# Expert slots filled from both ends: gather products of 160 columns in place of 256, turned one-hots of 132 in place of 260

## The chip, the cores and the metric

The kernel runs on one core of one Trainium2 chip. The metric is the device time in microseconds (us) of one execution. TensorE (PE) runs matrix products; its weight loads (PEld) are instructions of their own that overlap with products. VectorE (DVE) and ScalarE (ACT) read and write SBUF and PSUM; SyncE (SP) issues the DMAs. The granted clock of TensorE is given as a share of 2.4 GHz.

## What is computed

One step of a trunk with two layers over 256 tokens: 128 context tokens (group 0, the prompt) and 128 latent tokens (group 1), each 1024 wide, all in float32. Layer 0 mixes tokens with a convolution module, layer 1 with attention; after either comes the same mixture of experts, and this is what the change touches:

```python
def moe(h, router_w, router_bias, wg, wu, wd, sg, su, sd):
    scores = jax.nn.sigmoid(jnp.einsum('td,de->te', x, router_w, ...))
    ...
    _, eidx = lax.top_k(jnp.where(emask, choice, -jnp.inf), TOP_K)
    wsel = jnp.take_along_axis(scores, eidx, axis=1)
    wsel = wsel / jnp.sum(wsel, axis=-1, keepdims=True) * ROUTED_SCALE
    routed = routed_experts(x, eidx, wsel, wg, wu, wd)
    return (routed + swiglu(x, sg, su, sd)).reshape(B, L, D)
```

Each token goes to 8 of 64 experts; an expert is `(silu(x @ wg) * (x @ wu)) @ wd` with wg and wu of 1024x256 and wd of 256x1024, so its weights are 3 MB. All 64 experts' weights are read in either layer.

## The kernel before

**Routing.** All 256 tokens' scores are computed at once; VectorE picks each token's 8 experts as a 0/1 matrix `sel` (tokens on partitions, 64 experts along the row, one matrix for each token group). TensorE multiplies `sel` with triangular and full matrices of ones (L793 to L797) to get, in PSUM bank `ps[7]`, how many tokens with the same expert stand ahead of each token. VectorE turns this into `rank` (L1565, L1567): the token's slot at that expert, group 0 first and group 1 behind it. An expert has 64 slots. Experts with more tokens than slots get further turns, "overflow" turns, whose number and list VectorE and TensorE work out between L1569 and L1599 (`novc`, `novb`, `ovl`, `table`); TensorE works on the shared expert's hidden rows (L783) between these small steps.

**Pairs.** Experts are worked in pairs, so that two experts' 64 slots fill 128 partitions. There are 32 pairs, and a 33rd for two overflow turns that always runs; further overflow pairs run only where `nov > 2`. Both the 32 pairs and the 33rd run through the same code, `pair`, most of them in a loop of 4 pairs (two pairs' slots, 256 of them, are gathered together). For each pair TensorE does, in this order:

- gate_up (L861): the pair's 128 gathered rows times the gate and up weights, in full float32, 32 instructions of 512 columns; the two experts share the array's columns.
- gather, first half (L834): 8 products. Gathering is itself a product: weights are a 128x128 block of the token rows, split in a rounded float32r part `h_hi` and a float32r rest `h_lo`; the moving operand is `hot`, one-hot columns that say which token stands in which slot. One product covers all 256 slots of two pairs for one token group and one of the parts, so 2 groups x 2 parts add up in PSUM for each of 8 blocks of the width; half of the blocks are done beside one pair, half beside the next.
- combine (L901): 16 products of 256 columns that add the pair before into the 256 tokens' sums.
- hidden_t (L878): two transposes of the hidden rows.
- gather, second half (L834): 8 more products.
- combine_t (L870): the one-hots of the next pair, turned to slots x tokens, by two products with `turn`, a matrix of 260 columns for each token group: identity in the group's own 128 columns, zeros in the other's 128, and 4 columns of routing weights between them. The two products add up in the last 260 columns of bank `PT`.
- down (L890): hidden rows times the down weights, 16 instructions.

ScalarE copies the gathered blocks out (L1204), applies silu (L1210) and writes the rounded part of the pair's output (L1216). VectorE makes the one-hots four pairs ahead (L1612) from `rank` and a row of numbers 0 to 63, copies the routing weights in between the turned identities (L1620), copies the turned one-hots out (L1626), and multiplies silu by up (L1638).

**Weights.** SyncE issues the weights' DMAs into a ring of four experts: when gate_up of a pair has ended, the gate and up weights of the pair two later (4 DMAs of 1 MB, L392), and when its down has ended, the down weights of that pair (2 DMAs of 1 MB, L396). Behind the last expert of layer 0 the same queue carries the 6 MB of the attention's weights (L518) and the first units of 1 MB of the adaLN weights (L368), whose products (L541) are among the first that TensorE does in layer 1.

Of the kernel before, what the change touches and what calls it, by code (L numbers as in the profile page):

```python
# [31 lines left out]
G = 2  # L32
# [16 lines left out]
MAXOVF = TT * TOPK // (SLOTS + 1) + 1  # L49
OVF_PAIRS = MAXOVF // 2  # L50
# [8 lines left out]
TURN = TT + 4  # L59
# [47 lines left out]
def build_kernel(nc, x_prompt, x_sample, cache_k, cache_v, c, c_ctx, ada_w, ada_b, norm_mix, norm_ffn,  # L107
# [4 lines left out]
    with ExitStack() as ctx:  # L112
# [49 lines left out]
        novc = sb("novc", [NE, 8])  # L162
# [20 lines left out]
        eye = rounded("eye", [P, 3 * P + 8], rw_at, 0)  # L183
        turn = [eye[:, 0:TURN], eye[:, P + 4:P + 4 + TURN]]
        wst = eye[:, P:P + 2 * (P + 4)].rearrange("p (g c) -> p g c", g=G)[:, :, 0:4].rearrange(
# [46 lines left out]
        def block_of(i, k):  # L232

            q, second = i // 2 % 2, i % 2
            if q == 0:
                return 8 * second + k
            return 4 * second + k + (4 if k >= 4 else 0)

# [295 lines left out]
        def _(pe):  # L534
# [59 lines left out]
            for l in range(L):  # L594
# [199 lines left out]
                pe.matmul(ps[7][:, NE:2 * NE], ubf[:, 1, :], selb[:, 0, :], start=True, stop=False)  # L794
                pe.matmul(ps[7][:, NE:2 * NE], ubf[:, 0, :], selb[:, 1, :], start=False, stop=True)
                for g in range(G):
                    mm = pe.matmul(ps[7][0:NE, 2 * NE:2 * NE + 2], selb[:, g, :], ubf[:, 1, 0:2],  # L797
                                   start=(g == 0), stop=(g == G - 1))
# [474 lines left out]
        def _(dve):  # L1273
# [67 lines left out]
            for l in range(L):  # L1341
# [213 lines left out]
                if l == 0:  # L1555
                    dve.tensor_scalar(eye[:, P + 4:2 * P + 4], ident, 0.0, None, ALU.mult)
                    for o in (0, 2 * P + 8):
                        dve.tensor_copy(eye[:, o:o + P], ident)
# [241 lines left out]
```

## Time and profile before

| what | value |
|---|---|
| time, median of 3 runs (lowest to highest) | 1396.32 us (1395.77 to 1397.83) |
| time of the profiled execution | 1399.58 us |
| its span, first to last instruction | 1397.8 us |
| PE busy | 1351.7 us, 97% of the span |
| VectorE, ScalarE busy | 449.4 us (32%), 305.6 us (22%) |
| mean granted clock | 0.979 |
| DMA in the 40 slices of the experts' stages | 9 tenths or more, 401 to 424 GB/s |

The profiled execution's own time is 1.8 us above its span, and 3.3 us above the median of the runs. The page gives busy time by engine, the span in 40 slices, the chain of work that ended last, and groups of instructions with their mean duration. An instruction's duration holds the whole way through the engine; products that follow each other overlap, so that what a product costs is read from how far apart their starts are, or from the chain, not from its duration.

### The profile page before, as it was taken

The page shows a single profiled execution, that of the slowest core. Times are in us where ns is not written, and L with a number is a line of the kernel's source. Part 1 is how long each engine was busy: PE and PEld are TensorE (multiplying, and loading weights), DVE is VectorE, ACT ScalarE, POOL GpSimd, SP SyncE. Part 2 cuts the span into 40 slices and gives each one's busy share as a digit, 9 for nine tenths or more (in the row PEclk, how much of TensorE's full clock was granted, in tenths as well). Part 3 has the DMA queues.
Part 4 walks back from the last instruction along what each step waited for, and adds up shares of the span by engine and source line. Part 5 has one row for each costly group of instructions (what it writes and reads, how often), then busy time and mean ns, then how long its engine had stood idle before and what let it go on. Part 6 is the DMA issues. An engine that isn't in the chain of part 4 may idle for free.

```text
span 1397.8 us, 19630 instructions
## 1 busy us (share of the span) xinstructions
PE 1351.7 (97%) x7334; PEld 781.2 (56%) x7334; DVE 449.4 (32%) x1488; ACT 305.6 (22%) x641; POOL 21.1 (2%) x34
## 2 busy tenths in 40 slices
PE   5998999999999999999989999999999999999997
PEld 2776784555555555555534687655555555555554
DVE  1698262222222222222134525222222222222212
ACT  2343231121121111111131423111111111111111
POOL 0041000000000000000000000000000000000000
PEclk8899999999999999999999979999999999999999
DMA  9986879699999999999992726569999999999991
GB/s 346 396 335 276 307 313 370 248 407 418 421 420 418 412 417 418 421 409 424 418 417 88 308 111 251 217 251 401 419 422 421 414 416 414 421 419 408 418 420 65
DMA packets 83011, 499.46 MB, mean 357 GB/s; under 512 B 10697, under 2 KB 19569, under 8 KB 26128
## 3 DMA queue, kind: packets, MB, share of 16 engines
q1 hardware_dynamic: 82384, 498.57, 87.4%
q8 instruction: 31, 0.51, 0.1%
q10 hardware_dynamic: 576, 0.22, 0.1%
q14 instruction: 20, 0.16, 0.0%
HBM read 497.45 MB, written 1.31 MB: 357 GB/s over the span
## 4 chain that ended last, share of the span: by engine, by line
PE 92%; DVE 4%; DMA 2%; issue 1%; ACT 1%; SPq 0%; DVEq 0%; ACTq 0%
PE ps L861 33%; PE ps L890 17%; PE ps L834 10%; PE ps L901 9%; PE ps L566 4%; PE ps L613 3%; PE ps L653 3%; DVE ps L1365 2%; DMA ring<-in_conv_w_dram 2%; PE ps L541 2%; PE ps L783 2%; PE ps L878 1%; PE ps L870 1%; PE ps L719 1%; PE ps L821 1%; PE ps L555 1%
## 5 line engine op out<-in xcount | busy, mean ns | idle before, releaser
L861 PE MATMUL ps<-ring,hT 128*64 128x512 f32 x2048 | 453.3, 594 | 1.2 <-ACT hT L1204 0.9
L861 PEld LDWEIGHTS ps<-ring,hT 128*64 128x64 f32 x2048 | 166.1, 137 | 281.6 <-issue 276.7
L890 PE MATMUL ps<-ring,W 128*64 128x512 f32 x1024 | 233.8, 598 | 1.0 <-DVE W L1643 1.0
L1649 DVE TENSOR_TENSOR ypart<-ps,ypart 128x512 fp32r<-128x512 f32 x132 | 91.3, 692 | 187.1 <-ACT ypart L1216 187.1
L834 PE MATMUL ps<-hot,h_hi 128*128 128x256 f32 x544 | 146.6, 304 | 0.6 <-ACT hT L1204 0.6
L1638 DVE SCALAR_TENSOR_TENSOR vec<-silu_h,W,ps 128x256 f32<-128x256 f32 x66 | 31.7, 480 | 354.7 <-ACT silu_h L1210 354.7
L901 PE MATMUL ps<-comb,ypart 128*128 128x256 f32 x1056 | 138.5, 284 | 0.6 <-DVE ypart L1649 0.6
L890 PEld LDWEIGHTS ps<-ring,W 128*64 128x64 f32 x1024 | 67.8, 136 | 119.5 <-issue 109.6
L834 PE MATMUL ps<-hot,h_lo 128*128 128x256 f32 x544 | 134.4, 281 | 0.0
L1204 ACT ACTIVATE hT<-ps 128x512 f32<-128x512 f32 x136 | 81.2, 597 | 240.3 <-PE ps L834 240.3
L901 PEld LDWEIGHTS ps<-comb,ypart 128*128 128x128 f32 x1056 | 131.4, 191 | 4.2 <-DVE ypart L1649 2.6
L834 PEld LDWEIGHTS ps<-hot,h_hi 128*128 128x128 f32 x544 | 103.1, 189 | 53.0 <-issue 51.9
L1216 ACT ACTIVATE ypart<-ps 128x512 fp32r<-128x512 f32 x132 | 78.9, 598 | 179.8 <-PE ps L890 179.8
L1210 ACT ACTIVATE silu_h<-ps 128x256 f32<-128x256 f32 x66 | 25.4, 385 | 423.3 <-PE ps L861 423.3
L834 PEld LDWEIGHTS ps<-hot,h_lo 128*128 128x128 f32 x544 | 103.0, 189 | 0.1
L1643 DVE COPY W<-ps 128x256 f32<-128x256 f32 x66 | 28.0, 425 | 153.2 <-PE ps L878 153.2
L1365 DVE SCALAR_TENSOR_TENSOR ps<-W,vec,ps 128x256 f32<-128x256 f32 x168 | 66.9, 481 | 0.0
L613 PE MATMUL ps<-hT,ring 128*128 128x256 f32 x256 | 59.7, 394 | 1.5 <-DMA ring<-in_conv_w_dram 1.5
L613 PEld LDWEIGHTS ps<-hT,ring 128*128 128x128 f32 x256 | 50.1, 198 | 13.2 <-issue 3.4
L1626 DVE CAST comb<-ps 128x128 fp32r<-128x128 f32 x132 | 32.2, 286 | 66.4 <-PE ps L870 66.4
L1612 DVE TENSOR_SCALAR hot<-cst,rank 128x64 fp32r<-128x64 f32 x256 | 46.7, 246 | 0.0
L653 PE MATMUL ps<-S,hT 128*128 128x512 f32 x96 | 41.8, 593 | 0.0
(208 smaller groups left out, 914.4 us busy)
## 6 DMA issues: line engine op xcount, KB each, us to landing
ring<-in_exp_w_gate_dram SPq DMA_DIRECT2D x128, 1024.0 KB, 8.3
ring<-in_exp_w_up_dram SPq DMA_DIRECT2D x128, 1024.0 KB, 10.5
ring<-in_exp_w_down_dram SPq DMA_DIRECT2D x128, 1024.0 KB, 10.3
ring<-in_ada_w_dram SPq DMA_DIRECT2D x26, 1024.0 KB, 16.5
S<-in_ada_w_dram SPq DMA_DIRECT2D x22, 1024.0 KB, 13.9
S<-in_attn_wqkv_dram SPq DMA_DIRECT2D x1, 6144.0 KB, 25.5
ring<-in_conv_w_dram SPq DMA_DIRECT2D x4, 1024.0 KB, 19.6
ring<-in_conv_w_dram SPq DMA_DIRECT2D x2, 2048.0 KB, 15.6
```

Of the source, the lines that this page charges most:

```text
L566: mm = pe.matmul(banks[b][:, h * TT:(h + 1) * TT], w[:, k, (2 * b + h) * P:(2 * b + h + 1) * P], x[:, k, :], start=(k == 0), stop=(k == KC ...
L613: mm = pe.matmul(ps[3 + n % 4][:, h * TT:(h + 1) * TT], w1[:, k, h * D + n * P:h * D + (n + 1) * P], hT[:, k, :], start=(k == 0), stop=(k ...
L653: mm = pe.matmul(ps[3 * g + n][:, :], hT[:, k, g * T:(g + 1) * T], wqkv[:, k, n * 512:(n + 1) * 512], start=(k == 0), stop=(k == KC - 1))
L834: mm = pe.matmul(bank[:, kk * TT:(kk + 1) * TT], held, hot[:, buffer, g, :], start=(n == 0), stop=(n == 2 * 2 - 1))
L861: mm = pe.matmul(PGU[64 * b:64 * b + 64, :].rearrange("p (h f) -> p h f", h=2), xg[:, block_of(layout, k), 64 * b:64 * b + 64], gate_up_of ...
L890: mm = pe.matmul(bank[64 * b:64 * b + 64, :], hidT[:, j, 64 * b:64 * b + 64], down_of(w[b])[:, j, n * 512:(n + 1) * 512], start=(j == 0), ...
L901: pe.matmul(acc[k // 2][:, (k % 2) * TT:(k % 2 + 1) * TT], ypart[:, part, k * P:(k + 1) * P], comb[:, par, :], start=False, stop=False, sk ...
L1204: act.activation(blocks[:, lo // step_m:lo // step_m + pairs, lo % step_m:lo % step_m + 2, :], bank[:, :].rearrange("p (k m s) -> p m k s" ...
L1216: act.activation(half_of(0, h), bank[:, :], ACT.Copy).then_inc(act_yhi[l], 1)
L1365: ins = dve.scalar_tensor_tensor(last, x, tap, o, ALU.mult, ALU.add)
L1612: ins = dve.tensor_scalar(hot[:, c // 2 % 2, g, 128 * (c % 2) + 64 * b:128 * (c % 2) + 64 * b + 64], iota, column(rank[:, g, :], 2 * i + b ...
L1649: dve.tensor_tensor(half_of(1, h), bank[:, :], half_of(0, h), ALU.subtract).then_inc(dve_ylo[l], 1)
```

## The change

Slots are given out from both ends. Group 0's tokens of an expert take slots 0, 1, 2 and so on, up to slot 39 at most; group 1's take slots 63, 62, 61 and so on downward, to slot 24 at the lowest, and no lower than group 0's count. So a token group only ever stands in 40 of an expert's 64 slots, and a gather product for one group streams 4 pieces of 40 columns (`spanned`) in place of all 256. What the tokens' groups have beyond that goes to overflow turns, which take 32 more from either group. The turned one-hots of the two groups go to overlapping ranges of 132 columns, so the zero halves of `turn` are left out; the four columns in which they overlap are the weights, that add up as before.

On TensorE the rank products no longer add up the two groups (one count each), and there are as many as before. On VectorE the rank computation grows, and the overflow ranks move behind the first pair's `combine_copy` (`overflow_ranks`).

```diff
+SPAN = 40
+HALF = SLOTS // 2
+OVF_PAIRS = (3 * TT * TOPK // (SPAN + 2 * HALF + 1) + 3) // 4 * 2
+MAXOVF = 2 * OVF_PAIRS
...
-TURN = TT + 4
+TURN = P + 4
...
-                pe.matmul(ps[7][:, NE:2 * NE], ubf[:, 1, :], selb[:, 0, :], start=True, stop=False)
-                pe.matmul(ps[7][:, NE:2 * NE], ubf[:, 0, :], selb[:, 1, :], start=False, stop=True)
+                pe.matmul(ps[7][:, NE:2 * NE], ubf[:, 0, :], selb[:, 1, :], start=True, stop=True)
+                pe.matmul(ps[7][:, 2 * NE:3 * NE], ubf[:, 1, :], selb[:, 0, :], start=True, stop=True)
...
+                def spanned(v, g):
+
+                    at = 0 if g == 0 else SLOTS - SPAN
+                    return v.rearrange("p (e s) -> p e s", s=SLOTS)[:, :, at:at + SPAN]
...
-                            mm = pe.matmul(bank[:, kk * TT:(kk + 1) * TT], held, hot[:, buffer, g, :],
-                                           start=(n == 0), stop=(n == 2 * 2 - 1))
+                            mm = pe.matmul(spanned(bank[:, kk * TT:(kk + 1) * TT], g), held, spanned(hot[:, buffer, g, :], g),
+                                           start=(n == 0), stop=(n == 2 * 2 - 1), skip_group_check=True)
...
-                        mm = pe.matmul(PT[:, 512 - TURN:512], hot[:, buffer, g, 2 * SLOTS * par:2 * SLOTS * (par + 1)],
-                                       turn[g], start=(g == 0), stop=(g == G - 1))
+                        o = 512 - TT - 4 + P * g
+                        mm = pe.matmul(PT[:, o:o + TURN], hot[:, buffer, g, 2 * SLOTS * par:2 * SLOTS * (par + 1)],
+                                       turn[g], start=(g == 0), stop=(g == G - 1), skip_group_check=True)
...
-                dve.tensor_scalar(rank[:, :, :], rank[:, :, :], -1.0, None, ALU.add)
-
-                step(dve.tensor_copy(novc[:, 0:1], ps[7][0:NE, 2 * NE:2 * NE + 1]))
-                for n in range(3):
-                    ins = dve.tensor_scalar(novc[:, 1 + n:2 + n], novc[:, 0:1], (n + 1) * SLOTS + 0.5, None, ALU.is_gt)
+
+                dve.tensor_scalar(lowest, ps[7][:, 2 * NE:3 * NE], float(SLOTS - SPAN), float(SPAN), ALU.max, ALU.min)
+                dve.tensor_scalar(rank[:, 0, :], rank[:, 0, :], -1.0, None, ALU.add)
+                dve.tensor_scalar(rank[:, 1, :], rank[:, 1, :], -1.0, float(SLOTS), ALU.mult, ALU.add)
...
+                dve.tensor_scalar(over[:, 0, :], rank[:, 0, :], SPAN - 0.5, float(SLOTS), ALU.is_gt, ALU.mult)
+                dve.tensor_tensor(over[:, 1, :], lowest, rank[:, 1, :], ALU.is_gt)
...
+                for n in range(4):
+                    ins = dve.tensor_scalar(novc[:, 8 + n:9 + n], novc[:, 5:6], n * HALF + 0.5, None, ALU.is_gt)
                 step(ins)
-                step(dve.tensor_tensor(novc[:, 4:5], novc[:, 1:2], novc[:, 2:3], ALU.add))
-                step(dve.tensor_tensor(novc[:, 4:5], novc[:, 4:5], novc[:, 3:4], ALU.add))
+                step(dve.tensor_reduce(novc[:, 4:5], novc[:, 8:12], AX_X, ALU.add))
...
                 combine_copy(0, 0)
+                overflow_ranks()
```

TensorE inside the experts' loop, second half of a gather and the turned one-hots, before (`hot`: one-hots, `h_hi` and `h_lo`: the token rows' two parts, `eye`: the turned identities, `vec`: the hidden rows):

```order
L878 MATMUL ps<-cst,vec 128x128 x2
L834 MATMUL ps<-hot,h_hi 128x256
L834 MATMUL ps<-hot,h_lo_50 128x256
...
L870 MATMUL ps<-eye,hot 128x260 x2
L890 MATMUL ps<-ring,W 64x512 x8
```

and after:

```order
L892 MATMUL ps<-cst,vec 128x128 x2
L847 MATMUL ps<-hot,h_hi 128x4x40
L847 MATMUL ps<-hot,h_lo_50 128x4x40
...
L884 MATMUL ps<-eye,hot 128x132 x2
L904 MATMUL ps<-ring,W 64x512 x8
```

The order and the number of products stay; the gather products go from 256 columns to 4 pieces of 40, the turned one-hots from 260 to 132.

VectorE in the routing, from the ranks to `novb`, which TensorE waits for (`wt` holds `lowest`), before:

```order
L1565 SCALAR_TENSOR_TENSOR rank<-ps,sel 128x128
L1567 TENSOR_SCALAR rank<-rank 128x128
L1569 COPY novc<-ps 64x1
L1571 TENSOR_SCALAR novc<-novc 64x1 x3
L1573 TENSOR_TENSOR novc<-novc 64x1
L1574 TENSOR_TENSOR novc<-novc 64x1
L1575 TENSOR_SCALAR novb<-cst,novc 64x128
```

and after:

```order
L1578 SCALAR_TENSOR_TENSOR rank<-ps,sel 128x128
L1581 TENSOR_SCALAR wt<-ps 128x64
L1582 TENSOR_SCALAR rank<-rank 128x64
L1583 TENSOR_SCALAR rank<-rank 128x64
L1584 COPY novc<-ps 64x2
L1585 TENSOR_SCALAR W<-rank 128x64
L1586 TENSOR_TENSOR W<-wt,rank 128x64
L1587 TENSOR_SCALAR novc<-novc 64x1
...
L1593 TENSOR_SCALAR novc<-novc 64x1 x4
L1595 TENSOR_REDUCE novc<-novc 64x1
L1596 TENSOR_SCALAR novb<-cst,novc 64x128
```

9 instructions became 18, all ahead of the same `novb`. The 17 instructions of `overflow_ranks` come later, between the first pair's `combine_copy` and its `hidden`, where VectorE had none.

## Rows read from the trace of the kernel before

**Rows 1.** The page, busy time by engine.

```profile
PE 1351.7 (97%) x7334; PEld 781.2 (56%) x7334; DVE 449.4 (32%) x1488; ACT 305.6 (22%) x641; POOL 21.1 (2%) x34
```

**Rows 2.** Chain of one pair in layer 0: start us, us, what.

```profile
403.79 6.98 PE ps L861 x32
410.77 1.15 PE ps L834 x8
...
414.08 0.95 PE ps L834 x8
415.03 0.24 PE ps L870 x2
415.27 3.58 PE ps L890 x16
```

**Rows 3.** The page's groups: xcount | busy us, mean ns | idle before.

```profile
L834 PE MATMUL ps<-hot,h_hi 128*128 128x256 f32 x544 | 146.6, 304 | 0.6 <-ACT hT L1204 0.6
L1638 DVE SCALAR_TENSOR_TENSOR vec<-silu_h,W,ps 128x256 f32<-128x256 f32 x66 | 31.7, 480 | 354.7 <-ACT silu_h L1210 354.7
```

**Rows 4.** Timeline of PEld as a gather begins: start us, us.

```profile
410.70 0.19 PEld L834 LDWEIGHTS ps<-hot,h_hi 128*128 128x128 f32 x1 [0.81 <-issue]
410.81 0.19 PEld L834 LDWEIGHTS ps<-hot,h_lo 128*128 128x128 f32 x1
```

**Rows 5.** Timelines and chain where other products with 128x128 weights stand in a row.

```profile
785.38 1.86 PEld L719 LDWEIGHTS ps<-ring,W 128*128 128x128 f32 x16 [0.84 <-DVE W L1469]
180.33 1.47 PE L772 MATMUL ps<-cst,hT 128*128 128x128 f32 x12
862.59 3.46 PE ps L783 x16
```

**Rows 6.** Layer 0's loop: stretch, PE and PEld busy of L834, clock, DMA share, GB/s.

```profile
260.00:690.00 430.00, 69.63 (x464) 58.61 (x464) 1.00 1.00 415
```

**Rows 7.** Issue times on SP's queue, timeline.

```profile
320.48 0.33 SPq L392 DMA_DIRECT2D ring<-in_exp_w_gate_dram  x1
365.65 0.33 SPq L392 DMA_DIRECT2D ring<-in_exp_w_gate_dram  x1
668.90 0.38 SPq L392 DMA_DIRECT2D ring<-in_exp_w_up_dram  x1
1349.30 0.38 SPq L392 DMA_DIRECT2D ring<-in_exp_w_up_dram  x1
```

**Rows 8.** DMA issues at 320.5, 365.7, 668.9, 1349.3, 704.1: us to landing.

```profile
ring<-in_exp_w_gate_dram SPq DMA_DIRECT2D x1, 1024.0 KB, 7.1
ring<-in_exp_w_gate_dram SPq DMA_DIRECT2D x1, 1024.0 KB, 6.7
ring<-in_exp_w_up_dram SPq DMA_DIRECT2D x1, 1024.0 KB, 13.3
ring<-in_exp_w_up_dram SPq DMA_DIRECT2D x1, 1024.0 KB, 14.0
ring<-in_ada_w_dram SPq DMA_DIRECT2D x1, 1024.0 KB, 18.6
```

**Rows 9.** Chain: pair 33's gate_up in both layers, the second adaLN products.

```profile
690.27 6.87 PE ps L861 x32
1370.64 6.87 PE ps L861 x32
721.97 3.57 PE ps L541 x32
```

**Rows 10.** Timeline of layer 0's routing on VectorE, and who uses `novb`.

```profile
189.50 0.28 DVE L1565 SCALAR_TENSOR_TENSOR rank<-ps,sel 128x128 f32<-128x128 f32 x1
190.81 0.28 DVE L1575 TENSOR_SCALAR novb<-cst,novc 64x128 bf16<-64x128 f32 x1
192.97 0.20 PE L802 MATMUL ps<-ubf,novb 64*128 64x64 bf16 x1
```

**Rows 11.** Timeline of VectorE behind the place of `overflow_ranks`; its idle time in brackets.

```profile
216.60 0.48 DVE L1638 SCALAR_TENSOR_TENSOR vec<-silu_h,W,ps 128x256 f32<-128x256 f32 x1 [6.38 <-ACT silu_h L1210]
```

More of the change, by code:

```diff
@@ L161, in build_kernel @@
         ovrank = sb("ovrank", [P, G, NE])
-        novc = sb("novc", [NE, 8])
+        novc = sb("novc", [NE, 16])
         novb = sb("novb", [NE, P], BF16)
@@ L182, in build_kernel @@
         wt2 = rounded("wt2", [P, G, 2, NE], rstd_at, 0)
-        eye = rounded("eye", [P, 3 * P + 8], rw_at, 0)
-        turn = [eye[:, 0:TURN], eye[:, P + 4:P + 4 + TURN]]
-        wst = eye[:, P:P + 2 * (P + 4)].rearrange("p (g c) -> p g c", g=G)[:, :, 0:4].rearrange(
+        eye = rounded("eye", [P, 2 * TURN], rw_at, 0)
+        turn = [eye[:, g * TURN:(g + 1) * TURN] for g in range(G)]
+        wst = eye[:, P:P + 4 * G].rearrange("p (g c) -> p g c", g=G).rearrange(
             "p g (s b) -> p g s b", s=2)
@@ L237, in block_of @@
             return 4 * second + k + (4 if k >= 4 else 0)
+        lowest = wt[:, 0, :]
+        over = W[:, 1408:1536].rearrange("p (g e) -> p g e", g=G)
+        excess = W[:, 4352:4480].rearrange("p (g e) -> p g e", g=G)
+        turns = W[:, 4480:4608].rearrange("p (g e) -> p g e", g=G)
         logits = W[:, 1920:2048]
@@ L1555, in _ @@
                 if l == 0:
-                    dve.tensor_scalar(eye[:, P + 4:2 * P + 4], ident, 0.0, None, ALU.mult)
-                    for o in (0, 2 * P + 8):
-                        dve.tensor_copy(eye[:, o:o + P], ident)
+                    for g in range(G):
+                        dve.tensor_copy(eye[:, (TURN + 4) * g:(TURN + 4) * g + P], ident)
                 step(dve.tensor_copy(wt2[:, :, 0, :], wt[:, :, :]))
@@ L1588, in shared_half @@
                     dve.tensor_tensor(shh[:, 2 + j, :], shh[:, j, :], SHARED[2 + j], ALU.mult).then_inc(sh_hid, 1)
-                step(dve.tensor_scalar(ovrank[:, 0, :], ps[7][:, 0:NE], 1.0, float(SLOTS), ALU.subtract, ALU.mult))
-                step(dve.tensor_copy(ovrank[:, 1, :], ovrank[:, 0, :]))
-                dve.tensor_tensor(ovrank[:, :, :], ovrank[:, :, :], rank[:, :, :], ALU.add).then_inc(dve_ov[l], 1)
+                for g in range(G):
+                    dve.tensor_scalar(ovrank[:, g, :], ps[7][:, 0:NE], float(SLOTS), None, ALU.mult)
                 step(dve.tensor_tensor(endc[:, :], novc[:, 4:5], ps[7][0:NE, NE:NE + 1], ALU.add))
@@ L1650, in y_rest, with overflow_ranks @@
                                           ).then_inc(dve_ylo[l], 1)
+                def overflow_ranks():
+                    dve.tensor_scalar(excess[:, 0, :], rank[:, 0, :], float(-SLOTS - SPAN), None, ALU.add)
+                    step(dve.scalar_tensor_tensor(excess[:, 1, :], rank[:, 1, :], AWAY + 1.0, lowest, ALU.add, ALU.subtract))
+                    step(dve.tensor_scalar(excess[:, 1, :], excess[:, 1, :], -1.0, None, ALU.mult))
+                    dve.tensor_tensor(ovrank[:, 0, :], ovrank[:, 0, :], excess[:, 0, :], ALU.add)
+                    step(dve.tensor_tensor(ovrank[:, 1, :], ovrank[:, 1, :], excess[:, 1, :], ALU.subtract))
+                    for n in range(1, 4):
+                        for g in range(G):
+                            ins = dve.tensor_scalar(turns[:, g, :], excess[:, g, :], n * HALF - 0.5,
+                                                    float(HALF if g == 0 else 3 * HALF), ALU.is_gt, ALU.mult)
+                        step(ins)
+                        step(dve.tensor_tensor(ovrank[:, :, :], ovrank[:, :, :], turns, ALU.add))
+                    dve.tensor_scalar(ovrank[:, 1, :], ovrank[:, 1, :], SLOTS - 1.0, None, ALU.add)
+                    step(dve.tensor_scalar(turns, excess[:, :, :], -0.5, -FAR, ALU.is_lt, ALU.mult))
+                    dve.tensor_tensor(ovrank[:, :, :], ovrank[:, :, :], turns, ALU.add).then_inc(dve_ov[l], 1)
                 def overflow_experts(j):
```

15 lines of the change are left out of this document (10 added, 5 removed).

## The prediction

> **What bounds the kernel now.** I read the page first: PE is busy for 97% of the span [rows 1]. The DMA engines are as full: in the experts' loop their share is 1.00, at 415 GB/s [rows 6]. With two full resources the question is which of them ends last, and the chain of one pair answers it: seven pieces of PE, none of anything else (the two not shown are the combine products and the transposes), from 403.79 to 418.85 us, 15.06 us in all [rows 2]. PE waits for nothing in the loop. Of these 15.06 us the two half gathers take 1.15 + 0.95 us, and the turned one-hots 0.24. The first half gather is 0.20 us longer than the second: it follows gate_up, whose products lie otherwise in the array. There are 1088 gather products in both layers (544 with h_hi in their group and as many with h_lo), and 66 pairs, 33 in either layer [rows 3].
>
> The DMA queue is not behind, but near. The gate weights issued at 320.48 land 7.1 us later, at 327.6; those issued at 365.65, three pairs later, land 6.7 us later, at 372.35 [rows 7, 8]. In between the queue delivers a pair's 6 MB in 44.75 / 3 = 14.92 us, while PE takes 15.06, so the queue gains 0.14 us a pair, and now and then loses it again, since over the loop it moves 415 GB/s [rows 6] and 6.29 MB in 14.92 us would be 422. What keeps PE from feeling it is the lead: the last gate and up weights of layer 0 are issued at 668.90 and land at 682.2, PE uses them at 690.27, 8.1 us later; in layer 1 they land at 1363.3 and are used at 1370.64, 7.3 us later [rows 7 to 9].
>
> **Gather products, the one large term.** In a row of them one costs 0.95 / 8 = 0.119 us [rows 2]. If the columns alone set that, 160 in place of 256 would make it 0.074. I don't believe it, because each product brings its own 128x128 weights, and what these cost is seen where the columns are few. At L719 products have 64 columns in full float32, and their weight loads, as long as the gather's (0.19 us), start (1.86 - 0.19) / 15 = 0.111 us apart; the transposes of L772 with 128 columns stand (1.47 - 0.27) / 11 = 0.109 us apart, 0.27 being a lone one's length [rows 5]. And where a gather begins, before its products are in step, its own first two weight loads start 0.11 us apart [rows 4]. So weights cost 0.109 to 0.111 us whatever the columns, and the gather stands just above, since 256 columns cost about as much as the weights and each holds up the other. I take 0.111, from the row whose weight loads are as long: 8 ns less a product, 10 ns at the other end, nothing at the near end, should the 0.119 be a cost of float32r weights. Below 0.109 I see no row; the other end of the range upward is a rival, below. One product of 16 (the first behind gate_up) is spaced by something else and gains nothing. In each layer there are 544 / 16 = 34 times 15 products: 34 x 15 x 8 ns = 4.1 us.
>
> The Trainium skill (TensorE: Matmul & The Clock Gate, "LDWEIGHTS (loading the stationary operand)") speaks against the size of this change: a weight load takes its columns divided by 1.2 GHz however long the product is, 107 ns for 128. The trace agrees within 2 to 4 ns; by the page's figure a product would save 12 ns and a layer 7 us, by the columns 26.
>
> **Turned one-hots.** Two a pair, 0.24 / 2 = 0.120 us each, from 260 to 132 columns: by the same floor 0.111, so 33 x 2 x 9 ns = 0.6 us a layer. Together 4.7 us a layer, or 0.14 us a pair: a pair would take 14.92 us, exactly what the DMA queue delivers in its clean stretches. So the queue's lead isn't used up, but it doesn't grow either.
>
> **Layer 0's gain is cut at its end.** The same queue carries, behind the experts, the attention's weights and the adaLN units. The eighth unit is issued at 704.1 and lands 18.6 us later, at 722.7 [rows 8]; its product is the last quarter of the 3.57 us from 721.97, so it begins at 724.65 [rows 9], with 2.0 us to spare. PE can come earlier only by this plus what the DMA stream itself moves. The stream starts behind pair 3's gate_up, by when PE has done 80 gather products, 0.7 us earlier with the turned ones; in the next pairs the queue still fills up, which gives perhaps 0.3 more. So 2.0 + 1.0 = 3.0 us of the 4.7 remain in layer 0. At the end of layer 1 nothing is queued behind, and 7.3 us of lead take the 4.7 in full.
>
> **Routing on VectorE.** From the ranks to `novb` it takes 189.50 to 191.09 [rows 10]. There are 9 more instructions, of 64 columns or one, which by these rows' pace (1.31 us for the 8 starts from the first to the last) add 9 x 0.16 = 1.5 us at most. TensorE takes `novb` at 192.97, after the shared expert's products, 1.9 us after it is ready: hidden, with 0.4 us left. What is queued behind on VectorE is the float32r rest `h_lo`, which the gathers need only behind the rest of the shared expert's products (two more rounds of them and its down). If an instruction cost twice as much, 1.1 us a layer would show. The list of 60 in place of 32 entries lies on the path (VectorE writes `table`, TensorE waits): 28 elements more, by the 480 ns for 256 in VectorE's row [rows 3] 0.05 us a layer. In `overflow_ranks` 17 instructions, by 0.16 to 0.28 us each (the pace and the longest row of the routing) 2.7 to 4.8 us, lie in the 6.38 us before 216.60 in which VectorE waits for ScalarE's silu [rows 11]: free, and what would be late next is `hidden` of the first pair, with 1.6 us left. The one-hots are made from `rank` as before, the ACT copies and their sizes stay.
>
> **The sum.** 3.0 + 4.7 - 0.1 = 7.6 us off the profiled execution: its span from 1397.8 to 1390.2, its time from 1399.58 to 1392.0. The runs' median is 3.3 us below that execution, so 1396.3 - 7.6 = **1388.7 us**, 0.5% faster. With 0.109 and layer 0 not cut it is 2 x 5.8 = 11.6, 1384.7.
>
> **Rival 1, nothing: a gather product stays at 0.119 us.** Its 0.119 are then the price of float32r weights, not of two things of equal length. For it: the turned one-hots have other operands and the same price, 0.120 [rows 2], and no float32r product of this trace is narrower than 256 columns. Against it: the 0.11 us between the first two loads [rows 4]. Time 1396.4.
>
> **Rival 2, slower: narrow float32r products lose their rate.** That a 256-column product in float32r costs 0.119 and one in full float32 costs two instructions of 3.46 / 16 = 0.216 us, 0.432 [rows 5], shows that float32r has a fast way through the array. Nothing in the trace shows that this way is open below 256 columns, or to columns in four pieces. If it is not, 160 columns cost 160/256 of 0.432, 0.270 us, and the turned ones 0.223: 1088 x 0.151 + 132 x 0.103 = 178 us more, **1575 us**, and PE alone sets the end, the DMA queue idling for 2.6 us a pair. It decides from 0.122 us a product on (that is 0.2%). The float32 products at L719 with 64 columns show no such fall, but they are another type. The Trainium skill (FP8 and Floating Point Precision, "TensorE Precision Notes") gives true float32 four passes through the array, which the 0.432 us agree with (four times 256 columns at 2.4 GHz); it states no rate for float32r, narrow or wide, so it takes nothing from this rival.
>
> **Rival 3, the DMA bound.** Weights are no floor and a product costs 0.074: PE would need 0.8 us less a pair, and the queue's 14.92 us would set the pace. The gain is then the lead of 7.3 us plus 2 to 4 us of an earlier start in layer 1, and some 5 in layer 0: about 1381. Rows 4 and 5 speak against it.
>
> **Rival 4, more work.** The new rule could send tokens to overflow turns that had room before. With the reference's inputs I counted the routing: one expert in either layer overflows by the old rule and one by the new, so the 33rd pair still holds them. A further pair would cost 15.06 us, 1404. Or a small loss from the pieces of 40 columns, of some us.
>
> **Chances.** Forecast 0.60; rival 1 0.20; rival 2 0.13; rival 3 0.03; rival 4 and the pieces 0.04. About 0.2% (2.8 us) is what a measurement can tell from no change. Faster by more than that: the forecast but for its lowest sizes, and rival 3, 0.60. Within: rival 1 and the rest of the forecast, 0.23. Slower: rivals 2 and 4, 0.17. The range goes from the deepest form of the forecast to rival 1 with the runs' spread, 1384.5 to 1398, and leaves out rivals 2, 3 and 4, 0.20.
>
> **What the profile after would show.** In a pair's chain the second half gather would be 0.89 us for 0.95, the pair 14.92 for 15.06, and no other piece changed. Weight loads of the gather would start 0.11 us apart without a break. By rival 1 the chain repeats row by row; by rival 2 the half gather is over 2 us and the DMA share falls to 0.85. The DMA queue's share stays 1.00, its GB/s in the loops rise from 415 to about 418, and the last gate and up weights land 3 to 6 us before their use. In layer 1's beginning PE or its weight loads would wait about a microsecond for an adaLN unit. `novb` would be ready just ahead of TensorE; an idle time there of over 0.4 us would prove me wrong on the routing.

## The result, and the profile after

The changed kernel takes **1384.46 us**, median of 4 runs (1383.01 to 1385.87). The kernel before took 1397.07 us beside it (4 runs, 1395.77 to 1398.77). The ratio is 0.9909, 95% interval 0.9896 to 0.9923: 12.6 us less, where 7.6 were forecast. The profiled execution took 1383.01 us, its span is 1381.2 us. Measured once more beside the last experiments, the same kernel gave 1384.47 us (4 runs), ratio 0.9902 (0.9887 to 0.9917) to the kernel before, which took 1397.86 us there.

The chain of one pair in layer 0 (start us, us, what), which answers to [rows 2]:

```profile
405.96 1.05 PE ps L847 x8
407.02 1.95 PE ps L915 x16
408.97 0.24 PE ps L892 x2
409.21 0.86 PE ps L847 x8
410.07 0.21 PE ps L884 x2
410.28 3.58 PE ps L904 x16
```

L847 is the gather (1.15 and 0.95 us before, 1.05 and 0.86 now), L884 the turned one-hots, L904 the down projection. From the first gather to down it is 4.32 us, 4.50 before. Over both loops, as the mean of some 50 pairs in each trace, measured between the starts of the pieces, in ns:

| from the start of ... to ... | before | after |
|---|---|---|
| first half gather, combine | 1053 | 962 |
| combine, hidden_t | 1924 | 1946 |
| hidden_t, second half gather | 157 | 163 |
| second half gather, turned one-hots | 1026 | 940 |
| turned one-hots, down | 333 | 303 |
| down, next gate_up | 3580 | 3579 |
| gate_up, first half gather | 7018 | 7018 |
| a pair | 15089 | 14910 |

179 ns a pair, times 66 pairs, is 11.8 us. In time between the layers' marks (start of gate_up of the 1st and of the 33rd pair) layer 0 went from 481.0 to 475.3 us and layer 1 from 481.1 to 475.4, 5.8 and 5.7 less.

Where the gather begins, on the timeline of PEld (answers to [rows 4]), the weight loads now stand 0.11 us apart without a break, into the combine (L915):

```profile
405.89 0.19 PEld L847 LDWEIGHTS ps<-hot,h_hi 128*128 128x128 f32 x1 [0.81 <-issue]
406.00 0.19 PEld L847 LDWEIGHTS ps<-hot,h_lo 128*128 128x128 f32 x1
...
406.56 0.19 PEld L847 LDWEIGHTS ps<-hot,h_hi 128*128 128x128 f32 x1
406.67 0.19 PEld L847 LDWEIGHTS ps<-hot,h_lo 128*128 128x128 f32 x1
406.78 0.30 PEld L915 LDWEIGHTS ps<-comb,ypart 128*128 128x128 f32 x2
```

The loop window of layer 0 (of the gather's line alone: PE and PEld busy, clock, DMA share, GB/s), which answers to [rows 6], and one of SP's issues with the DMA view's time to landing, as [rows 7, 8] have it:

```profile
260.00:690.00 430.00, 63.43 (x456) 55.55 (x456) 1.00 1.01 422
```

```profile
661.00 0.38 SPq L400 DMA_DIRECT2D ring<-in_exp_w_up_dram  x1
ring<-in_exp_w_up_dram SPq DMA_DIRECT2D x1, 1024.0 KB, 12.3
```

The last up weights of layer 0 land at 673.3, and the chain has their gate_up at 682.03: 8.7 us of lead, not less than the 8.1 of before.

### The profile page after: what moved, and what is told of

Same layout as the page of the kernel before. It is cut to its first block, busy times and chain, and to the rows that moved or that the text cites. A ratio compares the mean times of both kernels' runs of the same rounds, so it can differ in the third digit from the quotient of the medians.

```text
span 1381.2 us, 19679 instructions
## 1 busy us (share of the span) xinstructions
PE 1335.2 (97%) x7334; PEld 770.2 (56%) x7334; DVE 457.2 (33%) x1537; ACT 305.4 (22%) x641; POOL 21.0 (2%) x34
## 4 chain that ended last, share of the span: by engine, by line
PE 92%; DVE 4%; DMA 2%; ACT 1%; issue 1%; SPq 0%; DVEq 0%; ACTq 0%
PE ps L874 33%; PE ps L904 17%; PE ps L847 9%; PE ps L915 9%; PE ps L574 4%; PE ps L621 3%; PE ps L661 3%; PE ps L549 3%; DVE ps L1379 2%; PE ps L791 2%; DMA ring<-in_ada_w_dram 2%; PE ps L892 1%; PE ps L829 1%; PE ps L727 1%; PE ps L884 1%; PE ps L563 1%
## 5 line engine op out<-in xcount | busy, mean ns | idle before, releaser
L904 PE MATMUL ps<-ring,W 128*64 128x512 f32 x1024 | 233.9, 599 | 1.0 <-DVE W L1662 1.0
L915 PE MATMUL ps<-comb,ypart 128*128 128x256 f32 x1056 | 140.1, 285 | 0.6 <-DVE ypart L1668 0.6
L847 PE MATMUL ps<-hot,h_hi 128*128 128x160 f32 x544 | 135.9, 289 | 0.5 <-ACT hT L1218 0.5
L847 PEld LDWEIGHTS ps<-hot,h_hi 128*128 128x128 f32 x544 | 104.8, 193 | 52.8 <-issue 51.9
L915 PEld LDWEIGHTS ps<-comb,ypart 128*128 128x128 f32 x1056 | 130.4, 191 | 4.2 <-DVE ypart L1668 2.6
L904 PEld LDWEIGHTS ps<-ring,W 128*64 128x64 f32 x1024 | 67.9, 137 | 115.5 <-issue 109.6
L847 PE MATMUL ps<-hot,h_lo 128*128 128x160 f32 x544 | 128.2, 275 | 0.0
L847 PEld LDWEIGHTS ps<-hot,h_lo 128*128 128x128 f32 x544 | 104.5, 192 | 0.1
```

The source lines that it names most:

```text
L847: mm = pe.matmul(spanned(bank[:, kk * TT:(kk + 1) * TT], g), held, spanned(hot[:, buffer, g, :], g), start=(n == 0), stop=(n == 2 * 2 - 1) ...
L904: mm = pe.matmul(bank[64 * b:64 * b + 64, :], hidT[:, j, 64 * b:64 * b + 64], down_of(w[b])[:, j, n * 512:(n + 1) * 512], start=(j == 0), ...
L915: pe.matmul(acc[k // 2][:, (k % 2) * TT:(k % 2 + 1) * TT], ypart[:, part, k * P:(k + 1) * P], comb[:, par, :], start=False, stop=False, sk ...
```

## The experiments

Twelve kernels in the first part ask what each piece of the change is worth, what a gather product costs, and how fast the DMA queue can go; four more ask where a rest of the gain comes from. "Pair" is always the mean as in the table above. Runs for which no number of executions is given were executed once, so a difference of 1 to 2 us between two of them says nothing; what is read from their traces, in ns a pair, repeats within some 5 ns from trace to trace of one kernel.

### The kernel before once more

> The kernel before once more, beside the next three on one chip, for its trace. Theory A (the DMA queue delivers what TensorE's pace asks for and is no bound): a pair takes 15.09 us on average and the expert weights land 15.09 / 6 = 2.51 us apart on average, with a median of 2.48. Theory B (the queue is the bound at its own rate and that rate differed between the two profiled executions, 2.48 and 2.45 us a MB in the median): the median landing distance here moves toward 2.45 and the pair gets shorter with it, under 15.0 us.

1397.38 us; a pair 15.090 us, the median distance of landings 2.483 us, the layers 481.1 us each: theory A. Between the layers it was 197.3 us, 199.3 in the trace on which the prediction rests. So outside the pairs one trace differs from another by some 2 us, inside them by less than 2 ns a pair.

### Routing alone

```diff
-                    return v.rearrange("p (e s) -> p e s", s=SLOTS)[:, :, at:at + SPAN]
+                    return v
...
-TURN = P + 4
+TURN = TT + 4
```

> The changed kernel's slots and VectorE work, with the gather products at 256 columns and the turned one-hots at 260 again: the routing part alone. Theory A (all of the gain is TensorE's shorter products, the added VectorE work is hidden): within 1 us of the kernel before, pair 15.09 us. Theory C (a part of the 12.6 us comes from elsewhere, such as fewer steps between rank and gather): 2 to 4 us faster than before.

1395.86 us (10 runs; ratio 0.9990, 0.9981 to 1.0000), a pair 15.083. The routing costs nothing that shows; where its 1.2 us of gain come from is told below (the ring's place).

### The turned one-hots alone, the gather alone

The first has only `spanned` undone, the second only `TURN`.

> As the run with the routing alone, but the turned one-hots at 132 columns; the gather stays at 256. Theory A: 0.03 us a pair less, 15.06 us, 2 us faster than before in all. If narrow float32r products had a price of their own, it would be seen here at 132 columns: slower than before.

> As the changed kernel, but the turned one-hots at 260 columns: the gather's part alone. Theory A: 0.15 us a pair less than before, 14.94 us, 10.5 us faster than before in all, so that this and the turned one-hots alone add up to the whole change. Rival: the two parts do not add up, since the DMA queue takes over at about 14.92 us a pair.

Turned alone: 1390.99 us (4 runs; 0.9954, 0.9937 to 0.9971), a pair 15.020. Gather alone: 1388.84 us (4 runs; 0.9936, 0.9919 to 0.9953), a pair 14.981. Against the routing alone that is 63 ns for the two turned products, where 18 were forecast, and 102 ns for the 16 gather products, where 120 were. With both it is 173, 8 ns more than the sum, and taken off last the gather gives 110 ns and the turned products 71: neither takes from the other. The piece from the turned one-hots to down went from 333 to 267 ns in the one, and from 371 to 303 in the other.

### What is the floor of a gather product?

Two kernels: 16 slots per end (64 columns a product), and 160 columns with half of the weights' columns.

```diff
-                    at = 0 if g == 0 else SLOTS - SPAN
-                    return v.rearrange("p (e s) -> p e s", s=SLOTS)[:, :, at:at + SPAN]
+                    at = 0 if g == 0 else SLOTS - 16
+                    return v.rearrange("p (e s) -> p e s", s=SLOTS)[:, :, at:at + 16]
```

> Left out: half of the change's turn-around, nothing else: the changed kernel, but each gather product takes only 16 slots at its end of an expert, 64 columns in place of 160, so that the slots 16 to 47 of the second group of tokens are not gathered for the tokens that lie there. Theory A (the load of 128 columns of weights is the floor of a gather product): the products inside a half gather stay 0.110 to 0.112 us apart, and what falls is only the first spacing, that from the first product to the second, by the columns that are no longer streamed (96 at 2.4 GHz, 40 ns, from 180 and 159 ns to about 140 and 119), given back at the start of the next piece. A pair stays within 30 ns of the 14.91 us of the changed kernel. Theory B (columns still set part of the 0.111): inside a half gather the spacing falls below 0.105 us, down to 0.03 us at the most, and a pair by 16 x 6 ns or more, 0.1 us up to 1.2 us.

```diff
-pe.matmul(spanned(bank[:, kk * TT:(kk + 1) * TT], g), held, spanned(hot[:, buffer, g, :], g),
+pe.matmul(spanned(bank[0:64, kk * TT:(kk + 1) * TT], g), held[:, 0:64], spanned(hot[:, buffer, g, :], g),
```

> Left out: half of the gathered rows. The changed kernel, with its 160 columns a gather product, but each product holds only 64 of the 128 columns of weights, so that only 64 partitions of each gathered tile are computed. Theory A (0.111 us is the weight load of 128 columns): with 64 columns of weights the load is half as long, and the 160 columns set the spacing, 160 / 2.4 GHz = 0.067 us up to 0.075; a half gather is 7 x 0.04 = 0.28 us shorter, a pair 0.5 to 0.6 us, by as much as the DMA queue lets it. Rival (0.111 is a price of a float32r product of itself): the spacing stays at 0.111 and a pair at 14.91 us.

With 64 columns the products stay 112 ns apart and a pair takes 14.914 us (1383.44 us in all): nothing more to be had. With half of the weights they stand 75 ns apart (timeline of PEld of that kernel):

```profile
399.91 0.14 PEld L847 LDWEIGHTS ps<-hot,h_lo 128*64 128x64 f32 x1
399.99 0.14 PEld L847 LDWEIGHTS ps<-hot,h_hi 128*64 128x64 f32 x1
400.06 0.14 PEld L847 LDWEIGHTS ps<-hot,h_lo 128*64 128x64 f32 x1
400.14 0.13 PEld L847 LDWEIGHTS ps<-hot,h_hi 128*64 128x64 f32 x1
400.21 0.14 PEld L847 LDWEIGHTS ps<-hot,h_lo 128*64 128x64 f32 x1
```

So 112 ns is the load of 128 columns of weights, theory A in both. The pair fell to 14.51 us (1363.91 us), 0.40 and not 0.5 to 0.6. The first half gather gives the 0.31 us that its products are nearer together; in the second half the turned one-hots come 192 ns behind the last gather product, not 75, and down comes 368 ns behind them, not 303. Their weight loads stand idle for some 0.16 us there, and what they wait for is not settled. The pair is also shorter than the 14.72 us at which the queue turns out to deliver (below): TensorE lives on the lead of the weights, which is down to 0.8 us at the end of layer 0.

And what set the 118 ns of before? The 256 columns again, with half of the weights (`at` and `SPAN` undone, `held[:, 0:64]` kept):

> Left out: half of the gathered rows. The changed kernel with the 256 columns of before in each gather product, but with 64 of the 128 columns of weights. Theory A (a product costs the larger of its columns and its weight load, and the 0.118 us of before are columns of 256 and their load together): with the load out of the way the columns alone give 256 / 2.4 GHz = 0.107 us, up to 0.110. Rival (0.118 us is what 256 columns of float32r cost by themselves): 0.118 us whatever the weights.

They stand 117 ns apart in the mean, almost the 118 of whole weights (the run took 1386.58 us):

```profile
407.26 0.14 PEld L846 LDWEIGHTS ps<-hot,h_hi 128*64 128x64 f32 x1
...
407.85 0.14 PEld L846 LDWEIGHTS ps<-hot,h_lo 128*64 128x64 f32 x1
```

(0.59 us for five of them.) Theory A fell here: columns and load don't hold each other up; 256 columns of float32r cost 117 ns with half of the load too. With 75 ns for 160 that is 0.44 ns a column and some 5 ns, and the two costs meet, by this estimate from two points, near 244 columns.

### Why the turned one-hots gave four times their price

Of the two products, one at 132 and one at 260 columns, in either order.

```diff
-                                       turn[g], start=(g == 0), stop=(g == G - 1), skip_group_check=True)
+                                       turn[g][:, lo:hi], start=(g == 0), stop=(g == G - 1), skip_group_check=True)
```

> Nothing of the result is left out. The gather of the changed kernel, and of the two turned products of a pair the first has 132 columns, the second the 260 of before (the second, which stands right ahead of the down projection, is the wide one). Beside it stands the run with the gather alone, in which both have 260 columns, and from the start of the turned products to the start of down it takes 371 ns; with both at 132 columns 302 ns. Theory A (a product in front of one of its own kind costs the larger of weights and columns, the last one, in front of another kind, costs its columns in full): narrowing the first saves the 8 to 10 ns between 260 columns and a weight load, so 360 to 365 ns. Rival (each of the two saves half of the 69 ns): 336 ns.

> Nothing of the result is left out. The gather of the changed kernel, and of the two turned products of a pair the first has the 260 columns of before, the second, right ahead of the down projection, 132. Theory A (the last of a row, in front of another kind, costs its columns in full): narrowing the second saves 128 columns at 2.4 GHz, 53 ns, and a little more, so 308 to 316 ns from the start of the turned products to the start of down, beside the 371 ns of both wide. Rival (each of the two saves half): 336 ns.

From the turned products to down: 371 ns with both wide, 360 with the first narrow, 313 with the second narrow, 303 with both. The first product is worth 11 ns, the second 58, which is 128 columns at 0.44 ns and little more. The whole pairs agree: 14.981 us with both wide, 14.970 with the first narrow, 14.925 with the second, 14.910 with both. So the two differ by where the narrow product stands. The reason, which is argued and not shown by itself: the first is followed by a product with 128 columns of weights, whose load costs as much as its columns; the second by down, whose 64 columns of weights are, by the gather's 75 ns above, no floor, so that its columns are paid in full. One row doesn't fit this: in the run with half of the weights the last gather product of the first half stands only 0.08 us ahead of the combine, whose weights have 128 columns, and the combine is no longer for it:

```profile
400.28 0.24 PE L847 MATMUL ps<-hot,h_lo 128*64 128x160 f32 x1
400.36 2.11 PE L915 MATMUL ps<-comb,ypart 128*128 128x256 f32 x16
```

Nor was it tried whether down's full float32, which costs each of its products more, has the same effect as its narrow weights. So the two prices are shown, and their reason is open. The runs took 1388.14 and 1385.39 us. The chains of one pair, first narrow and then second narrow, turned products (L884) and down (L904):

```profile
412.15 0.27 PE ps L884 x2
412.42 3.58 PE ps L904 x16
```

```profile
411.08 0.22 PE ps L884 x2
411.30 3.58 PE ps L904 x16
```

### How fast can the DMA queue go?

Half of the combine's products, which takes 0.96 us a pair off TensorE, and the same with the ring moved:

```diff
-                        for part in range(2):
+                        for part in range(1):
```

```diff
+        pad = sb("pad", [P, 80])
         ring = sb("ring", [P, 4, EW])
```

> Left out: the low part of the combine, so its sum over a pair's slots is only to the precision of float32r. The changed kernel, with 8 of the 16 combine products of a pair: TensorE would need about 14.91 - 0.96 = 13.95 us a pair, which is less than the DMA queue has shown, and the queue must set the pace. Theory A (the queue's own pace for a pair's six transfers of 1 MB is the median distance of their landings, 2.45 us in this form of the kernel): 14.7 us a pair, with TensorE waiting for gate, up or down weights in every pair. Rival (the queue's pace is 14.92 us, as the prediction has it, and the changed kernel already stands at it): 14.9 us a pair, nothing gained on the changed kernel.

> Left out: the low part of the combine, as in the run beside it. The same kernel with an unused tile of 320 bytes a partition in front of the ring of expert weights, which puts the ring at 320 bytes behind a multiple of 512, where it stands in the kernel before, in place of a multiple of 512. Theory A (where the ring starts sets the queue's pace): 6 x 2.483 = 14.90 us a pair, 0.18 us more than the run beside it. Rival (the 2.483 and 2.452 us between landings come from something else in the change): the same pace as the run beside it.

The first took 1358.08 us, the second 1372.00. In the first dozen pairs of a layer TensorE doesn't wait: gate_ups start 13.92 us apart and use up the lead of the weights. From then on (402.07 us in layer 0 of the first kernel) gate_up waits in every pair for up weights, and the starts of two in a row give the queue's own pace, in the mean 14.72 us in the first kernel and 14.91 in the second. The pairs shown are 14.75 and 14.91 us apart:

```profile
475.63 7.09 PE L874 MATMUL ps<-ring,hT 128*64 128x512 f32 x32 [0.66 <-DMA ring<-in_exp_w_up_dram]
490.38 7.09 PE L874 MATMUL ps<-ring,hT 128*64 128x512 f32 x32 [0.72 <-DMA ring<-in_exp_w_up_dram]
```

```profile
480.45 7.09 PE L875 MATMUL ps<-ring,hT 128*64 128x512 f32 x32 [0.90 <-DMA ring<-in_exp_w_up_dram]
495.36 4.94 PE L875 MATMUL ps<-ring,hT 128*64 128x512 f32 x22 [0.89 <-DMA ring<-in_exp_w_up_dram]
```

Theory A holds in both, but for the waits that it had in every pair. Windows of layer 0's loop (busy of the five engines, clock, DMA share, GB/s), ring at a multiple of 512 bytes, then 320 behind:

```profile
260.00:660.00 400.00, 387.97 (x2102) 192.70 (x2099) 102.16 (x354) 76.42 (x138) 0.00 (x0) 1.00 1.01 427
```

```profile
260.00:660.00 400.00, 382.95 (x2080) 190.63 (x2080) 102.55 (x356) 76.68 (x138) 0.00 (x0) 1.00 1.01 422
```

The DMA share is 1.01 in both, as in the changed kernel, and 1.00 or 1.01 in the two traces of the one before: it hardly differs whether the queue sets the pace or waits for TensorE.

### The changed kernel with its ring moved

> Nothing is left out. The changed kernel with an unused tile of 320 bytes a partition in front of the ring of expert weights, which stands then at 320 bytes behind a multiple of 512, as in the kernel before. Theory A (where the ring starts sets the distance between landings, and TensorE sets the pace of the changed kernel): the median landing distance goes from 2.452 back to 2.483 us, and since six of these are 14.90 us and TensorE needs 14.91, the time stays within 1.5 us of the changed kernel, 1384 to 1386; a wait for weights may show in a few pairs. Rival (the place of the ring is part of the gain of the changed kernel, since the queue had fallen behind): 1387 us or more, and pairs of over 14.93 us.

1386.51 us (4 runs, 1386.25 to 1386.65; ratio 0.9925, 0.9907 to 0.9942), a pair 14.902 us, median distance of landings 2.483 us (2.452 in the changed kernel). Inside the pairs nothing, as theory A has it, but the time is 2.0 us above the changed kernel's, more than its 1.5. In the trace the first gate_up is 2.1 us later (208.6 for 206.6; 0.6 beside the 208.0 of the changed kernel's second trace), and between the layers TensorE waits 0.6 us for the eighth adaLN unit (chain, and the same product on PE's timeline):

```profile
697.62 20.80 DMA ring<-in_ada_w_dram
718.41 0.04 issue
718.46 1.07 PE ps L550 x8
```

```profile
718.46 1.07 PE L550 MATMUL ps<-ring,scT 128*32 128x512 f32 x8 [0.59 <-DMA ring<-in_ada_w_dram]
```

The lead is smaller too. The last up weights of layer 0 land 14.8 us behind their issue, at 677.6, and gate_up follows at 683.83, 6.2 us later (SP's timeline, DMA view, chain):

```profile
662.81 0.38 SPq L401 DMA_DIRECT2D ring<-in_exp_w_up_dram  x1
ring<-in_exp_w_up_dram SPq DMA_DIRECT2D x1, 1024.0 KB, 14.8
683.83 2.57 PE ps L875 x11
```

### Where a rest of the gain comes from: the ring's place

The list, `novc` and `table` lie ahead of the ring in SBUF and have grown. By this the ring moved from 320 bytes behind a multiple of 512 to 0 behind one (worked out from the sizes of the tiles ahead of it; no view shows places in SBUF). The kernel before with 192 bytes ahead of its ring:

```diff
+        pad = sb("pad", [P, 48])
         ring = sb("ring", [P, 4, EW])
```

> Nothing is left out. The kernel before with an unused tile of 192 bytes a partition in front of the ring, so that the ring starts at a multiple of 512 bytes, as it does in the changed kernel. Theory A (the place of the ring sets the queue's pace and is a small part of the gain, outside the pairs): the median landing distance goes from 2.484 to 2.452 us, a pair stays at 15.09 us (TensorE sets it), and the time falls by 1 to 2 us, to 1395 to 1396, all of it ahead of the first pair and between the layers. Rival (the distance of landings belongs to what the change does to the work): 2.484 us and no change of the time.

> The changed kernel once more, on the chip of the other runs of this call, so that its gain over the kernel before and over the kernel before with its ring moved are told apart: 12 to 13 us below the first, 10.5 to 12 below the second, by the 0.179 us a pair x 66 = 11.8 us.

Moved: 1396.10 us (11 runs), beside 1397.86 for the kernel before (15 runs); ratio 0.9988, 0.9979 to 0.9997. The distance of landings fell from 2.484 to 2.453 us, the pair stayed (15.083). In the traces most of the 1.8 us lie ahead of the first gate_up, which starts at 207.0 us, and at 208.4 and 209.1 in the two traces of the kernel before: in all traces of this case it starts at 205.8 to 208.1 with the ring at a multiple of 256 bytes (13 traces), at 208.3 to 209.1 elsewhere (5). The routing alone took as much, 1395.86, with its ring at the same place, so the routing itself costs nothing that shows. The changed kernel is 11.6 us below the moved one, which the pairs' 0.179 x 66 = 11.8 us account for, and 13.4 below the kernel before, a little more than the 12 to 13 expected.

Which starts are slow? The kernel with 8 combine products again, with 16 and with 64 words of `pad`:

> Left out: the low part of the combine, as in the two runs with 8 combine products a pair. The ring starts 64 bytes behind a multiple of 512 (0 bytes gave 1358.08 us and 2.445 us between landings, 320 bytes 1372.00 and 2.486). Theory A (any start that is not a multiple of 512 makes pieces that straddle such a line): as with 320 bytes, 2.48 to 2.49 us and 1370 to 1373 us. Rival (only certain starts are slow, or the effect grows with the distance): between the two, 2.45 to 2.47 us, 1358 to 1368 us.

> Left out: the low part of the combine, as in the run beside it. The ring starts 256 bytes behind a multiple of 512. Theory A (only multiples of 512 are fast): 2.48 to 2.49 us, 1370 to 1373 us. Rival (multiples of 256 are enough, 64 and 320 are not): 2.445 to 2.453 us, 1358 us.

| ring, bytes behind a multiple of 512 | time us | landings' median distance us | GB/s, 260 to 660 us |
|---|---|---|---|
| 0 | 1358.08 | 2.445 | 427 |
| 64 | 1372.66 | 2.484 | 422 |
| 256 | 1361.30 | 2.449 | 427 |
| 320 | 1372.00 | 2.486 | 422 |

Each of the four was executed once. The start at 64 came out by theory A, the one at 256 by the rival: 256 is as good as 0 in the loop, 64 and 320 are not. The 3.2 us between 0 and 256 lie for the most part outside the loops. A pad moves all tiles behind it too, among them `S`, the one-hots and the output parts; that the ring alone counts was not tried.

## Why the prediction was wrong

The sign and the mechanism of the gather were right, the size was not: 1384.46 us lies just below the range's 1384.5, 12.6 us of gain for 7.6. That it came so near the range's low end is luck: that end (1384.7) was made of gather and turned products at 0.109 us, which is not what happened. Step by step, with what each was to give in both layers and what it gave:

| step | forecast us | measured us |
|---|---|---|
| gather products | 8.2 | 6.7 to 7.3 |
| turned one-hots | 1.2 | 4.2 to 4.7 |
| layer 0 cut at its end | -1.7 | 0 (a wait of 0.6 with the ring at its old place) |
| routing, list | -0.1 | 0 |
| the ring's place | not seen | 1 to 2 |

**Gather, right in kind.** The weight load is the floor; rivals 1, 2 and 3 (0.119, over 0.122 and 0.074 us a product) are out, and so is rival 4, since the layers hold 33 pairs as before. The term was 0.9 to 1.5 us too large: the products stood 118.1 ns apart in the mean and now 111.6, so 6.5 ns each, where 0.119 and 0.111 had made 8 of it; two roundings in one direction. The reason given for the 0.119, that columns and weights of equal length hold each other up, was wrong: 256 columns cost 117 ns with half of the load too. The Trainium skill (TensorE: Matmul & The Clock Gate, "LDWEIGHTS (loading the stationary operand)") gives a load's time by its own columns alone, 128 / 1.2 GHz or 107 ns; the traces agree in kind, with 112 ns whether the product streams 160 columns or 64.

**Turned one-hots, the term that was mis-sized.** "Two a pair ... by the same floor 0.111, so 33 x 2 x 9 ns" took the floor of a row of gather products for both. It holds for the first of the two (11 ns measured). The second stands ahead of down, with its smaller weights, and there all 128 columns count: 58 ns. This is the step that failed, a term of 1.2 us that measured 4.2 to 4.7: 3 to 3.5 of the 5 us that the forecast missed are here. Why the columns count there is argued above and not shown. The chain of before could not show it, its piece of 0.24 us being cut in two equal prices; the product in front of a change of kind had to be costed by columns, as its far bound at least.

**Layer 0 not cut.** The step had the DMA stream set its own times: it was to move by 1.0 us only, while TensorE came 4.7 earlier. But in the kernel before the stream went at TensorE's pace. Every load waits for a slot of the ring that TensorE frees, and the mean distance of landings was 2.51 us (300 to 680 us), a sixth of a pair's 15.09, while the median, near the queue's own, was 2.484. When the pair became shorter the mean went to 2.49, a sixth of 14.91, and all that is queued behind moved with it. The eighth adaLN unit, issued at 695.83, landed 18.0 us later at 713.8, its product is the last quarter of the piece at 713.07 (answers to [rows 9]):

```profile
695.83 0.56 SPq L376 DMA_DIRECT2D ring<-in_ada_w_dram  x1
ring<-in_ada_w_dram SPq DMA_DIRECT2D x1, 1024.0 KB, 18.0
```

```profile
713.07 3.57 PE ps L549 x32
```

It begins at 715.75, with 1.9 us to spare, 2.0 before. The ring's new place has a share in this. With the ring where it was, six landings take 14.90 us, the queue only just follows, and TensorE does wait for this unit, 0.6 us on its timeline, where the forecast had about a microsecond. So the limit was the right one; what the step missed is that the stream would speed up with TensorE and, by the ring's place, a little beyond. That the limit is real is shown also by the kernel with 8 combine products, where the stream does set the times, and these eight products start 0.04 us after the unit's landing:

```profile
681.27 25.48 DMA ring<-in_ada_w_dram
706.76 0.04 issue
706.80 1.07 PE ps L549 x8
```

**The queue's floor.** "14.92 us, exactly what the DMA queue delivers" was right for a ring 320 bytes behind a multiple of 512 (14.91 measured) and no longer after the change, which put it at a multiple of 512: 14.72. The forecast of a lead that shrinks to 3 to 6 us failed with it: 8.7 us in layer 0 and 8.4 in layer 1, but 6.2 in layer 0 with the ring moved back. The loop's rate rose to 422 GB/s, not 418. Rival 3's price (about 1381 us for products at 0.074) rested on the same 14.92: the run with half of the weights, whose products stand 75 ns apart, took 1363.91 us.

**Routing, right.** From the ranks to the end of `novb` it now takes 187.16 to 189.89, 2.73 us for 1.59 ([rows 10]), 1.1 more where at most 1.5 were expected. TensorE takes `novb` 0.8 us after it is ready, where it was 1.9 before, so it doesn't wait:

```profile
187.16 0.29 DVE L1578 SCALAR_TENSOR_TENSOR rank<-ps,sel 128x128 f32<-128x128 f32 x1
...
189.61 0.28 DVE L1596 TENSOR_SCALAR novb<-cst,novc 64x128 bf16<-64x128 f32 x1
...
190.71 0.20 PE L810 MATMUL ps<-ubf,novb 64*128 64x64 bf16 x1
```

`overflow_ranks` lies in VectorE's idle time, which before the first pair's `hidden` went from 6.38 us [rows 11] to 2.87, 3.5 us for a forecast of 2.7 to 4.8:

```profile
214.13 0.48 DVE L1657 SCALAR_TENSOR_TENSOR vec<-silu_h,W,ps 128x256 f32<-128x256 f32 x1 [2.87 <-ACT silu_h L1224]
```

**A note on the first product.** From the first product of a half gather to its second it took 222 and 202 ns before and 180 and 159 after, 42 less, about what 96 columns cost; but the piece behind the gather is longer by 34 and 39 ns (gather alone against routing alone). So these columns for the most part only moved the row's end against its beginning, and 3 to 9 ns are left, as of any other product: 102 ns for 16 products are 6.4 each. The prediction had left the first product of 16 out.

**No version beats the changed one with all its work.** Narrower gather products give nothing more. What a shorter pair could still give is more than its distance to the queue's pace, 66 x (14.91 - 14.72) = 12.5 us: the lead of 8.4 to 8.7 us in either layer can be used up too, which makes some 30 us by estimate. The kernel with 8 combine products took 1358.08 us, 26.4 below the changed one, bought with the low part of the combine.

## What to carry to other kernels

Cost a narrower product by the larger of its columns and a weight load, and look at what stands behind it: in a row of products with full weights nothing is left below the load (112 ns here), but in this case the last one in front of products with small weights paid every column, and narrowing it was worth nine of the others (58 ns for 6.4). Where a product stands at such a border, take its columns in full as one bound. A DMA share of 1.00 doesn't tell whether the queue is the bound: compare the median distance of landings (near the queue's own: 2.445 us where the queue set the pace at 14.72 / 6 = 2.453) with the mean (the pace it is held to); where they differ, as 2.484 and 2.51 do, a faster engine pulls the transfers along and the lead stays. And a lead is a store: while it lasts, TensorE can run faster than the queue delivers. And see where a change in small tables puts the large DMA targets behind them.

## What the hardware showed that was not expected

- Where the ring and the tiles behind it start in SBUF sets the rate of 1 MB loads: 2.445 to 2.453 us each with the ring at 0 or 256 bytes behind a multiple of 512, 2.483 to 2.486 at 64 or 320. That is 1.4%, and 11 to 15 us of the time in the kernel with 8 combine products, where the queue is the bound for most of a layer.
- A float32r product of 256 columns costs 117 ns and one of 160 in four pieces 75 ns (weights of 64 columns), 0.44 ns a column, and 64 to 160 columns cost 112 ns with 128 columns of weights.
- The same 128 columns were worth 11 ns in one product and 58 in the next; the reason is open.
